# One view for the two parts of the softmax sum, and mLSTM denominators read straight from PSUM, on VectorE

## What is computed

```python
# attention, per block of 128 queries and head; s: masked scores, sink: one extra logit per head
p = softmax(concatenate([s, sink]))[..., :-1]
o = einsum(p, vv)
# mLSTM, per chunk
num = inter * einsum(qc, Cp) + einsum(qk, vc)
den = inter * einsum(qc, Np) + sum(qk)
h = num / maximum(abs(den), exp(-m_t))
# both layers
return x + concatenate([branch_1 * gate_1, branch_2 * gate_2]) @ w_out
```

## Time and profile before

| | us |
|---|---|
| median of 3 runs | 1647.64 (1647.1 to 1648.34) |
| span of the profiled execution | 1643.3 |
| PE busy in the span | 1620.9 (99%) |
| PEld busy | 1349.1 (82%) |
| DVE busy | 970.9 (59%) |
| ACT busy | 500.2 (30%) |
| POOL busy | 507.4 (31%) |

### The profile page before, as it was taken

How to read it: one execution, slowest core, us unless ns; L and a number is a source line. 1 busy time by engine, 2 the same in 40 slices (tenths; PEclk the granted TensorE clock), 3 DMA queues, 4 the chain that set the end, 5 groups by cost and what they waited for, 6 DMA issues and landing times.

```text
span 1643.3 us, 20929 instructions
## 1 busy us (share of the span) xinstructions
PE 1620.9 (99%) x7776; PEld 1349.1 (82%) x7776; DVE 970.9 (59%) x1607; ACT 500.2 (30%) x1221; POOL 507.4 (31%) x582
## 2 busy tenths in 40 slices
PE   8999999999999999999999999999999999999998
PEld 8888888788888888887888888888888888888886
DVE  2847336895634773688652276267774237446866
ACT  2001234452300133445320022345441012243632
POOL 9877675457436312333340001000043000100001
PEclk9999999999999999999999999999999999999999
DMA  8988688657888886875895567654498558654457
GB/s 271 346 292 272 223 297 251 213 181 267 297 306 307 309 321 233 252 251 191 324 352 194 192 237 280 212 165 139 146 370 298 193 190 301 249 187 138 138 183 304
DMA packets 184469, 405.47 MB, mean 247 GB/s; under 512 B 34704, under 2 KB 86416, under 8 KB 184368
## 3 DMA queue, kind: packets, MB, share of 16 engines
q1 hardware_dynamic: 162256, 378.85, 66.2%
q10 hardware_dynamic: 22112, 25.28, 5.0%
HBM read 309.64 MB, written 94.44 MB: 246 GB/s over the span
## 4 chain that ended last, share of the span: by engine, by line
PE 84%; DVE 9%; DMA 3%; ACT 2%; ACTq 1%; issue 1%; POOL 1%; SPq 0%; DVEq 0%; POOLq 0%
PE bank L787 13%; PE bank L789 12%; PE bank L788 12%; PE pair_a L787 4%; PE pair_a L788 4%; PE pair_a L789 4%; PE pair_b L787 4%; PE pair_c L787 4%; PE pair_c L789 4%; PE pair_c L788 4%; PE pair_b L788 4%; PE pair_b L789 4%; PE pair_a L1171 1%; DMA slot<-split_weights 1%; DMA h_lo<-split_weights 1%
## 5 line engine op out<-in xcount | busy, mean ns | idle before, releaser
L787 PE MATMUL bank<-h_hi,slot 128*128 128x512 f32 (+1 forms) x976 | 379.7, 389 | 4.9 <-DVE proj L2162 4.0
L789 PE MATMUL bank<-h_hi,slot 128*128 128x512 f32 (+1 forms) x976 | 378.1, 387 | 0.0
L788 PE MATMUL bank<-h_lo,slot 128*128 128x512 f32 (+1 forms) x976 | 377.6, 387 | 0.0
L787 PEld LDWEIGHTS bank<-h_hi,slot 128*128 128x128 f32 x976 | 184.3, 189 | 43.3 <-DVE proj L2162 5.6
L789 PEld LDWEIGHTS bank<-h_hi,slot 128*128 128x128 f32 x976 | 184.1, 189 | 37.9
L788 PEld LDWEIGHTS bank<-h_lo,slot 128*128 128x128 f32 x976 | 184.4, 189 | 36.1
L653 POOL TENSOR_TENSOR slot<-stages,slot 128x512 fp32r<-128x512 f32 x132 | 184.4, 1397 | 11.0
L624 POOL TENSOR_TENSOR rs<-sums,small 128x1 f32<-128x1 f32 x48 | 15.8, 330 | 539.7 <-ACT proj L1330 325.1
L651 POOL TENSOR_SCALAR slot<-stages 128x512 fp32r<-128x512 f32 x132 | 94.6, 716 | 102.9 <-issue 101.1
L787 PE MATMUL pair_a<-h_hi,slot 128*128 128x512 f32 x256 | 99.6, 389 | 0.0
L788 PE MATMUL pair_a<-h_lo,slot 128*128 128x512 f32 x256 | 99.6, 389 | 0.0
(11 more groups left out here) (459 smaller groups left out, 3512.0 us busy)
## 6 DMA issues: line engine op xcount, KB each, us to landing
slot<-split_weights SPq DMA_DIRECT2D x356, 512.0 KB, 4.1
split_weights<-slot SPq DMA_DIRECT2D x132, 512.0 KB, 4.3
slot<-combined_weights SPq DMA_DIRECT2D x76, 512.0 KB, 5.3
stages<-in_even_w_in SPq DMA_DIRECT2D x48, 256.0 KB, 4.4
stages<-in_odd_w_in SPq DMA_DIRECT2D x36, 256.0 KB, 3.7
stages<-in_even_w_out SPq DMA_DIRECT2D x32, 256.0 KB, 4.2
combined_weights<-keys SPq DMA_DIRECT2D x16, 512.0 KB, 4.2
combined_weights<-stages SPq DMA_DIRECT2D x32, 256.0 KB, 3.1
```

Of the source, the lines that this page charges most:

```text
L787: t.matmul(dst, l_hi, r_hi, start=start, stop=False)
L788: t.matmul(dst, l_hi, r_lo, start=False, stop=False)
L789: return t.matmul(dst, l_lo, r_hi, start=False, stop=stop)
```

## The change

```diff
@@ mem_post @@
                     dve.wait_ge(s_mb, b * 4 + c + 1)
-                    step(v.tensor_copy(den[:, 0, :].rearrange("p (b i) -> p b i", b=2), pair_c[:, :, ME:2 * ME + 2:ME + 1]))
+                    sync()
+                    sums_of_keys = pair_c[:, :, ME:2 * ME + 2:ME + 1]
+                    by_pair = lambda t: t.rearrange("p (b i) -> p b i", b=2)
+                    step(v.scalar_tensor_tensor(by_pair(den[:, 1, :]), sums_of_keys, -1.0, by_pair(cols[:, q, 2 * MH:3 * MH]),
+                                                ALU.mult, ALU.max))
                     for i in range(2):
                         last = v.scalar_tensor_tensor(state[:, i, :], state[:, i, :], inter_bc[q][:, i, P - 1:P],
                                                       banks[3][:, 129 * i:129 * i + 129], ALU.mult, ALU.add)
                     last.then_inc(s_mem_state, 1)
                     sync()
-                    link(v.scalar_tensor_tensor(den[:, 1, :], den[:, 0, :], -1.0, den[:, 0, :], ALU.mult, ALU.max))
-                    link(v.tensor_tensor(den[:, 1, :], den[:, 1, :], cols[:, q, 2 * MH:3 * MH], ALU.max))
+                    link(v.tensor_tensor(by_pair(den[:, 1, :]), sums_of_keys, by_pair(den[:, 1, :]), ALU.max))
                     link(v.reciprocal(den[:, 1, :], den[:, 1, :]))
@@ att_sum @@
                     r = inv_sum[:, p % 4, :]
-                    link(v.tensor_tensor(r, sm[:, p % 2, 8:12], sm[:, p % 2, 12:16], ALU.add))
+                    link(v.tensor_reduce(r, sm[:, p % 2, 8:16].rearrange("p (s j) -> p j s", s=2), AX.X, ALU.add))
                     v.reciprocal(r, r).then_inc(s_att_sum, 1)
```

## The result

The kernel became faster: median 1635.93 us of five runs (1634.54 to 1639.92) against 1647.1 of five runs of before (1646.11 to 1648.34), a ratio of 0.9934 [0.992, 0.9948], 10.9 us. A later measurement of the same kernel gave 0.9954 [0.9935, 0.9972], 7.6 us.

The account below looks back on a forecast made before the run. PE was taken to bound the kernel, so only its stalls behind DVE could be won: 0.3 + 0.8 + 1.6 + 1.7 + 0.05 = 4.45, say 4.4 us, from 1647.64 to 1643.2 us, range 1641.7 to 1647.3.

Parts of the forecast that it names:

- What bounds the kernel, and the mechanism: PE bounds the kernel; DVE operations with two SBUF operands wait for POOL, a reduction takes 0.16 us without that wait.
- The rival that the reduction waits too: In att_sum the reduction waits for POOL like the addition, giving 1647.6 us; chance 0.06.
- First stall, block 0: Block 0's attention: L2161 still waits for L653 but ends at 325.67, not 325.95; gain 0.3 of 1.35 us.
- Second stall: Block 0's attention: L2168 ends 0.58 us earlier, a second addition gives 0.2; together 0.8 of 1.33 us.
- the flat 0.2 for the second addition: Block 0, just ahead of the second stall: another 1.24 us addition, taken to give slightly less than the first stall's.
- The denominators: 16 chains in mem_post, each 0.20 us shorter; PE waits behind them only at L2012 in block 0; gain 0.05 us.
- Block 1: Block 1's attention: L2168 goes ahead of POOL's L694; gain 1.6 of the two stalls' 2.36 us.
- The clock: Behind block 1's pair of stalls, from 766 us: PE's granted clock no longer falls; gain 1.7 us.
- PE's later work is not paced by anything that stays put: After the stalls, weights are fetched as PE frees slots, so the kernel's end moves with PE.
- The wait only moves: Rival for block 1 and block 0's second stall: L2161 and L2168 take over the wait; gain 0.7, 1646.9 us; chance 0.32.
- The change makes DVE earlier in every step: Argument against the slower rival: DVE comes earlier in every step, never later.
- the collision in a new place: Rival for blocks 0 or 1: earlier DVE arrives just behind POOL, PE pauses twice; price 4.1, 1651.7 us; chance 0.05.

Follow-up runs that it names:

- the pair with and without a second operand in front of the sum: Changed kernel plus an unread small operation before att_sum's reduction: two-operand addition 1642.41 us, 0.9983 to before; one-operand reduction 1640.34 us, 0.9965.
- the reduction from the third piece on: Kernel before, with att_sum's reduction only from each block's third attention piece on, the addition kept in the first two: 1640.76 us, 0.9969 to before.
- the copy put back: Kernel before with the changed denominators, plus an unread copy from PSUM giving mem_post's chain its old length; att_sum's addition kept: 1645.62 us, 0.9998 to before.

## Why the prediction was right or wrong

**What bounds the kernel, and the mechanism: right.** DVE's small additions waited for POOL inside the instruction, the reduction of eight columns doesn't (154 ns median, 165 at most, 0.16 forecast), and the pair with and without a second operand in front of the sum differs by 2.1 to 3 us with all else equal. The rival that the reduction waits too is out.

**"First stall, block 0", gain 0.3, and "Second stall", 0.8: wrong, the steps that failed.** In the table they gave 2.0 and 1.9 us. The prediction took DVE's arrival in front of the first stall as that of before, and asked only what one shorter addition does there. That piece of arithmetic was correct, as the reduction from the third piece on shows (1.08 us left of 1.35). What it left out are L2117 and L2119 of each step, two more small operations with two SBUF operands. In each of the three steps ahead of the first stall one of them starts 0.01 to 0.11 us behind L653 in before and pays 1.2 to 1.3 us. An addition 0.76 us shorter in the first step puts the next of them in front of L653, and in each of the two following steps the pair then takes 0.6 to 0.7 us less, which the edit never touched. The view of groups hid this, as I looked in it for the lines that the diff names.

At the second stall those two are undisturbed in before, and the step that failed is another one: the flat 0.2 for the second addition, with L2151 at nothing. The first addition gave its 0.58. The earlier DVE then passed POOL at L2151 (0.7 us) and at the second addition, where nobody took over the wait of 1.1 us.

**"The denominators", 0.05: the term was mis-sized, for the same reason.** Measured 4.3 us alone; for the whole change the table has 1.6 at `mem_pre`, where the prediction held the first stall for one of a DMA and the second for 0.2 at most: they went from 1.14 to 0.62 and from 0.87 to nothing. 0.2 us less in the chain let L2122 pass L653 by 0.04 us and the first stall of the attention vanished, for which the prediction had no term. With the copy put back the gain is nothing.

**"Block 1", 1.6: right for the whole change, partly by luck.** L2171 came before L694 and the pair of stalls shrank from 2.36 to 0.24 us. But the term was worked out for the reduction, and with the reduction alone the pair still was 1.80 us; before's second trace has it at 1.65. Where DVE and POOL happen to meet in block 1 decided as much as the edit.

**"The clock", 1.7: right for this pair of executions (1.6), wrong as a fixed term.** Before has the fall in one of its two traces, so in a median it counts for part only.

**"PE's later work is not paced by anything that stays put": partly wrong.** 2.1 us came back in block 1 of this pair of executions as waits for weights' DMAs (`pair_a` 0.7 us at the place of 541 us, `pair_b` 1.51 where before waited 0.23 at 615 us): PE came sooner to slots that were still being filled. In the second pair it was 0.3 us, so this too is no fixed term.

**"The wait only moves"**, held at 0.32, is true of single places (L2164 1.39 and L2171 1.50 us, and L2161 1.49 in block 1 with the reduction alone) and false of the sum. "The change makes DVE earlier in every step" doesn't rule out the collision in a new place: it came in after at 754.38, where L2120 took 1.12 us behind L718 and before's L2117 at this place 0.16, but no pause of PE over 0.24 us followed.

What stays open: the share of each part in the median. The table explains one pair of executions, 7.5 us apart, while the ratios say 7.6 and 10.9 us (the medians 8.2 and 11.2) and single runs of before reach 5 us to either side of their median. Also open is which executions have the clock's fall, and whether a POOL operation as long as L653 that only writes would hold DVE.

## What to carry to other kernels

A tiny VectorE operation with two SBUF operands can cost eight times its own length beside a busy GpSimd, so where two small operands can be put side by side in one tile, a reduction over the view has only one and was free of it here. When you cost such an edit, follow the engine's arrival time through the next steps and list all operations that stand within a few tenths of a microsecond of the other engine's, not only the edited one: a chain 0.20 us shorter, which passed it by 0.04 us, was worth 4.3 us here. And take a second trace before counting an event such as a fall of the clock as a term of the sum.

## What the runs showed of the hardware

- Two engines that arrive within 0.04 us of one another: a later DVE waits for the whole operation of POOL, 1.25 us for four columns (307.02 in before) against 0.16 (307.52 with the denominators alone).
- A POOL operation with one input holds such a DVE operation too. In after L651 ran from 310.69 for 0.62 us, and L2122, begun at 310.85, took 0.47 and ended at 311.32.
- The reduction with eight columns to four takes 154 ns in the median, the addition of four and four 159 undisturbed. The Trainium skill ("VectorE: DVE Perf Modes", section "Rules for kernel authors") calls `tensor_reduce` the slowest operation of a hot path; at this size the trace doesn't show it.
- PE's wait for POOL at L653 was 0.4 to 1.0 us in some executions and 2.1 in others, whatever the kernel (0.5 and 2.1 in before's two traces, 0.4 and 2.1 in after's). It can add to the scatter of single runs.
